# NSA attention: adding the causal mask with VectorE in PSUM in place of mask products on TensorE

## The chip, the cores and the metric

The kernel runs on 1 core of one Trainium2 chip. The metric is the device time of one execution in microseconds, as the median of several runs.

## The reference, cut to what matters

The program is two transformer blocks in a row, all in float32, on 256 tokens (plus 256 context tokens in the second block) with width 1024. The change touches only the NSA mixer of the first block, and of that only the part with full scores: the selected branch and the window branch. With 256 tokens, four blocks of 64 keys and a top-4 choice, every block is chosen, and the window of 512 covers everything. So both branches are plain causal attention over the 256 keys, each with keys and values of its own:

```python
def _masked_softmax(s, mask):
    s = jnp.where(mask, s.astype(jnp.float32), -1e30)
    m = jnp.max(s, axis=-1, keepdims=True)
    p = jnp.where(mask, jnp.exp(s - m), 0.0)
    return p / jnp.maximum(jnp.sum(p, axis=-1, keepdims=True), 1e-30)
...
        ss = jnp.einsum('bqgrd,bgqkld->bqgrkl', qb, k_g).reshape(...) * scale
        ps = _masked_softmax(ss, mask_s).reshape(...)          # mask_s: kpos <= t
...
        pw = _masked_softmax(jnp.einsum('bqgrd,bkgd->bqgrk', qb, kwb) * scale, mask_w)
        o_win = jnp.einsum('bqgrk,bkgd->bqgrd', pw, vwb)
        return gb[..., 0:1] * o_cmp + gb[..., 1:2] * o_slc + gb[..., 2:3] * o_win
```

There are 16 query heads of 64 dimensions in 2 key/value groups. The second block has four mixers' code, of which two layers run: a GQA attention and an MLA attention, both without a mask.

## The kernel before, in words

The program is one block per engine (TensorE, ScalarE, VectorE, GpSimd, and SyncE for the loads), written out by hand. Engines meet by semaphores; each engine runs its instructions in the order in which they are written. The program is cut into phases, and at the end of each (`end_phase`) TensorE, ScalarE and VectorE wait for one another. Weights stream from memory into six slots of SBUF.

One helper, `attention`, exists once per engine (L723 for TensorE, L1386 for ScalarE, L1865 for VectorE) and is called for NSA, GQA and MLA. Its unit is a `Pair`: two heads (`e` = 0, 1) and one tile of 128 queries. In NSA there are 16 pairs: 4 groups of heads `j`, 2 key/value groups `u`, and 2 query tiles `qt`. A pair has two branches (selected and window), and its width per branch is `w = 128 * (qt + 1)`: an even pair (qt = 0) has 2 heads x 2 branches x 128 keys = 512 scores a row, an odd one (qt = 1) has 2 x 2 x 256 = 1024. Below they are the short and the wide pair. Each head has a PSUM bank of its own: pair p uses banks 0 and 1 if p is even, 2 and 3 if it is odd.

For step p the engines do, each in this order:

- TensorE: the scores of pair p (waits until the exponentials of pair p-2 have left the banks, `att_exp`), then the transposes of the probabilities of pair p-2 (L739; waits for `att_scaled` of it and for `att_PT` of the pair before it, which frees banks 4 and 5), then the products with the values of pair p-3 (L1021, and L1025 for the compressed branch; waits for `att_PT`).
- VectorE: the row maximum of pair p, read from both banks in one instruction (L1873; waits for `att_S`), then for pair p-1 the reciprocal of the sums, the gate and four multiplications (L1881, L1884, L1889), and after every second pair a copy of the output (L2151).
- ScalarE: the exponentials of pair p, four instructions with their sums (L1397; waits for `att_max`), then the copy of the transposed probabilities of pair p-2 from PSUM to SBUF (L1406; waits for `att_T`).

The mask: only the last 128 keys of each branch are on the diagonal. `scores` makes the score product (L1009) with `stop=False`, and then, for each head, multiplies the constant `mneg` (0 where key <= query, -1e30 elsewhere) with the identity, repeated for the two branches, onto the diagonal block of the same bank (L1013). A float32 product is two instructions in the trace, so L1009 and L1013 have four each per pair. The constant `trix` is 1 where row < column and 0 elsewhere; it lies in SBUF already. `NEG` is -1e30.

Of the kernel before, what the change touches and what calls it, by code (L numbers as in the profile page):

```python
# [18 lines left out]
ALU = mybir.AluOpType  # L19
# [3 lines left out]
P = 128  # L23
# [6 lines left out]
NEG = -1e30  # L30
# [155 lines left out]
def build(nc, dr):  # L186

    with ExitStack() as ctx:
# [6 lines left out]
        banks = ctx.enter_context(nc.psum_tensor("bank", [P, 8, 512], F32))  # L195
# [22 lines left out]
        def C(name, rows=P):  # L218
            o, w = CO[name]
            return consts[0:rows, o:o + w]  # L220
# [4 lines left out]
        def slot(s, w=SLOTW):  # L225
            return ring[:, s * SLOTW:s * SLOTW + w]
# [26 lines left out]
        ident, ones = C("ident"), C("ones")  # L253
# [79 lines left out]
        kk = [pl(2, T) for _ in range(NKV)]  # L333
# [9 lines left out]
        q_all = pl(KD, T)  # L343
# [24 lines left out]
        start = pl(NE)  # L368
# [239 lines left out]
        def _(pe):  # L608
# [3 lines left out]
            mm, tr = nc.tensor.matmul, nc.tensor.transpose  # L612
# [20 lines left out]
            def dot(out, lhs, rhs, k):  # L633

                for i in range(k):
                    last = mm(out, lhs(i), rhs(i), start=i == 0, stop=i == k - 1)  # L636
                return last
# [36 lines left out]
            def hn_block(k):  # L674
                pe.wait_ge(s["hn_ready"], n["hn_ready"] - KD + k + 1)
                return hn[:, k, :]
# [75 lines left out]
            for v in range(VT):  # L752
                r = min(P, VR - v * P)
                last = tr(bank[v][:, 0:r], vec_rows[0:r, v, :], ident[0:r, 0:r])
# [130 lines left out]
            for c in range(2):  # L885
                last = dot(bank[5][:, c * 80:(c + 1) * 80], lambda k: hn_block(k)[:, c * P:(c + 1) * P],
                           lambda k: w_small[:, k, :], KD)
# [30 lines left out]
            def kvw(sl, x):  # L918
                return lambda k: slot(sl)[:, k * 384 + x * P:k * 384 + (x + 1) * P]
# [7 lines left out]
            for br in range(2):  # L927
                for t in range(TT):
                    last = dot(bank[2][:, (br * 2 + t) * P:(br * 2 + t + 1) * P], lambda k: hn[:, k, t * P:(t + 1) * P],
                               kvw(3, 2 * br), KD)  # L930
# [6 lines left out]
            for g in range(NKV):  # L937
# [3 lines left out]
                last = mm(bank[g][:, :], dup, k_roped[:, 1:3, :], start=True, stop=True)  # L941
# [3 lines left out]
            for x in range(2):  # L945
                landed(1 - x)
                for hb in range(2):
                    o = (x * 2 + hb) * 2 * NCMP
                    last = dot(bank[7][:, o:o + 2 * NCMP],
                               lambda k: slot(1 - x)[:, k * HID + hb * P:k * HID + hb * P + P],  # L950
                               lambda k: blk[x][:, k, :], 16)
# [6 lines left out]
            for g in range(NKV):  # L958
                last = dot(bank[4][0:NCMP, 320 + g * DH:320 + (g + 1) * DH],
                           lambda k: hid[:, 2 + k, g * NCMP:(g + 1) * NCMP], lambda k: w_cmp2[:, k, P:P + DH], 2)  # L960
# [42 lines left out]
            def nsa_pair(j, u, qt):  # L1003
                w = P * (qt + 1)

                def scores(*out):
                    for e in range(2):
                        rows = slice(64 * e, 64 * e + 64)
                        mm(out[e][:, 0:2 * w], q_all[rows, 2 * j + u, qt * P:(qt + 1) * P], kk[u][rows, :, 0:w],  # L1009
                           start=True, stop=False)  # L1010
                    for e in range(2):
                        diag = out[e][:, 0:2 * w].rearrange("p (b k) -> p b k", b=2)[:, :, qt * P:w]
                        last = mm(diag, C("mneg"), ident.unsqueeze(1).to_broadcast([P, 2, P]), start=False, stop=True)  # L1013
                    return last

                def values(out, pt):
                    to = [out[64 * e:64 * e + 64, qt * P:(qt + 1) * P] for e in range(2)]
                    for x in range(2 * (qt + 1)):
                        br, kt = x // (qt + 1), x % (qt + 1)
                        for e in range(2):  # L1020
                            mm(to[e], v_tok[:, br, kt, u * DH:(u + 1) * DH], pt[:, e, x * P:(x + 1) * P],  # L1021
                               start=x == 0, stop=False)
                    for e in range(2):
                        c = (4 * u + 2 * e + qt) * P
                        last = mm(to[e], v_cmp[0:NCMP, u, :], ct[0:NCMP, j, c:c + P], start=False, stop=True)  # L1025
                    return last

                return Pair(scores, values, tiles=[x * P for x in range(2 * (qt + 1))])
# [12 lines left out]
            for t in range(TT):  # L1041
                last = dot(bank[0][:, t * 36:(t + 1) * 36], lambda k: hn[:, k, t * P:(t + 1) * P],
                           lambda k: w_route[:, k, :], KD)
            last.then_inc(s["route_pe"], 1)
            for t in range(TT):
                for k in range(KD):
                    last = tr(bank[2 + 2 * t + k // 4][:, (k % 4) * P:(k % 4 + 1) * P], hn[:, k, t * P:(t + 1) * P], ident)
# [88 lines left out]
            for l in range(2):  # L1136
                norm(T2)
                if l == 0:

                    landed(0)  # L1140
                    for t in range(4):
                        last = dot(bank[6 + t // 2][:, (t % 2) * T:(t % 2 + 1) * T], lambda k: hn_block(k)[:, t * P:(t + 1) * P],
                                   lambda k: slot(0)[:, k * T:(k + 1) * T], KD)
# [58 lines left out]
                else:  # L1202

                    landed(0)
                    for b in range(3):
                        last = dot(bank[1 + b][:, 0:T], lambda k: slot(0)[:, k * 384 + b * P:k * 384 + (b + 1) * P],
                                   lambda k: hn_block(k)[:, 0:T], KD)
# [72 lines left out]
                w = T2 if l == 0 else T  # L1280
# [463 lines left out]
        def _(ve):  # L1744
# [3 lines left out]
            V = nc.vector  # L1748
# [116 lines left out]
            def attention(pairs, per, done, output):  # L1865

                N = len(pairs)
                for p in range(N + 4):
                    if p < N:
                        u = pairs[p]  # L1870
                        x = 2 * (p % 2)
                        ve.wait_ge(s["att_S"], done + p + 1)
                        V.tensor_reduce(nmax[p % 3][:, :, 0:u.branches],  # L1873
                                        banks[:, x:x + 2, 0:u.branches * u.w].rearrange("p e (b k) -> p e b k", b=u.branches),
                                        AX.X, ALU.max, negate=True).then_inc(s["att_max"], 1)
                    if 1 <= p < N + 1:
                        t = p - 1
                        u = pairs[t]
                        ve.wait_ge(s["att_exp"], 2 * (done + t + 1))
                        fac = pfac[t % 3][:, :, 0:u.branches]  # L1880
                        V.reciprocal(fac, psum_[t % 3][:, :, 0:u.branches])  # L1881
                        ve.drain()
                        if u.gate is not None:
                            V.tensor_tensor(fac, fac, u.gate, ALU.mult)  # L1884
                            ve.drain()
                        for e in range(2):
                            for b in range(u.branches):
                                pb = probs[t % 3][:, e, b * u.w:(b + 1) * u.w]
                                last = V.tensor_scalar(pb, pb, fac[:, e, b:b + 1], None, ALU.mult)  # L1889
                        last.then_inc(s["att_scaled"], 1)  # L1890
                    if p >= 4 and (p - 4) % per == per - 1:
                        g = (p - 4) // per
                        ve.wait_ge(s["att_O"], done + p - 3)
                        output(g, bank[6 + g % 2]).then_inc(s["att_ev"], 1)
# [185 lines left out]
            for x, name in enumerate(("cmp_pe_k", "cmp_pe_v")):  # L2080
                pe_cols = cols[:, VO[name]:VO[name] + 16]
                for g in range(NKV):
                    src = bank[5 + x][:, g * T:(g + 1) * T].rearrange("p (c j) -> p j c", j=STRIDE)
                    for h in range(2):
                        rows = slice(64 * h, 64 * h + 64)
# [60 lines left out]
            def nsa_pair(j, u, qt):  # L2146
                gate = gsel[:, j, 8:24].rearrange("p (b n) -> p n b", b=2)[:, 4 * u + qt:4 * u + qt + 3:2, :]
                return Pair(branches=2, w=P * (qt + 1), gate=gate)

            attention([nsa_pair(j, u, qt) for j in range(4) for u in range(2) for qt in range(2)], 2, 0,  # L2150
                      lambda g, b: V.tensor_copy(o_t[:, g // 2 + 4 * (g % 2), :], b[:, 0:T]))  # L2151
            end_phase()
# [144 lines left out]
            for i in range(ITEMS + 2):  # L2297
# [6 lines left out]
                if i < ITEMS:  # L2304
                    x = i % 2
# [23 lines left out]
            for l in range(2):  # L2329
# [4 lines left out]
                if l == 0:  # L2334
# [24 lines left out]
                    for b in range(2):  # L2359
                        block_step(b, KVG)  # L2360
                    end_phase()
                    attention([Pair(branches=1, w=512 if t % 4 < 2 else 256) for t in range(32)], 4, 16,
                              lambda g, b: V.tensor_copy(o2[:, g, :], b))
                    end_phase()
                    gemm(2, 4, T2, 16, 1)
                else:
# [36 lines left out]
                    with ve.Fori(1, 4) as trip:  # L2403
                        for q in range(2):
                            heads(trip * 2 + q, q)
                    heads(8, 0)
                    end_phase()
                    attention([Pair(branches=1, w=512) for _ in range(16)], 2, 48,
                              lambda g, b: V.tensor_copy(o2x[:, g, :], b[:, 0:T]))
                    end_phase()  # L2410
                    gemm(2, 4, T, 16, 2)
                w = T2 if l == 0 else T
# [192 lines left out]
```

## Time and profile before

| | us |
|---|---|
| median of 3 runs | 2266.38 (2265.53 to 2266.64) |
| profiled execution, its own time | 2266.16 |
| its span, first to last instruction | 2264.4 |
| TensorE busy in the span | 2047.4 (90%) |
| VectorE busy | 1050.3 (46%) |
| ScalarE busy | 550.6 (24%) |
| mean granted TensorE clock, share of full | 0.951 |

Busy time is the time in which an engine executed something. The chain that ended last is followed back from the last instruction: at each step to what released it, or to the instruction before it on its engine; its shares say on which engine time went by. NSA attention fills the stretch from 494.6 to 568.6 us of the span.

### The profile page before, as it was taken

To read this page: it belongs to the slowest core of one execution; us is meant where nothing else is said; L and a number is where in the kernel's file an instruction comes from. 1 tells how busy PE (TensorE), PEld (TensorE's weight loads), DVE (VectorE), ACT (ScalarE), POOL (GpSimd) and SP (SyncE) were. 2 spreads that over 40 slices of the span, in tenths; PEclk is the share of its full clock that TensorE was granted. 3 is DMA by queue.
4 is the path that set the end of the run, shared out by engine and by line. 5 is a ranking of instruction groups with operands and counts; after the bars stand their busy time and mean duration, and the time that the engine had idled before them with its cause. 6 is when DMAs were issued, how large, how long until landed. Compare 5 with 4: busy or idle time off the path is not lost.

```text
span 2264.4 us, 27759 instructions
## 1 busy us (share of the span) xinstructions
PE 2047.4 (90%) x10184; PEld 1448.1 (64%) x10184; DVE 1050.3 (46%) x2090; ACT 550.6 (24%) x1095; POOL 61.4 (3%) x69
## 2 busy tenths in 40 slices
PE   6999897878986999997978979999999878999997
PEld 4888686855874555554435448888644445678886
DVE  3456565535722222223666247777697423523311
ACT  3333300025012111112136213323100123534410
POOL 0000000000000000000000001111000010000000
PEclk9999999689988999998989989999999989999999
DMA  9444465040453999951000102222476011034451
GB/s 386 154 183 186 182 272 233 19 186 1 186 227 140 425 424 422 420 207 79 0 38 1 56 19 93 82 84 93 187 278 243 36 35 61 1 114 158 154 198 44
DMA packets 39081, 357.13 MB, mean 158 GB/s; under 512 B 4295, under 2 KB 8526, under 8 KB 9934
## 3 DMA queue, kind: packets, MB, share of 16 engines
q1 hardware_dynamic: 38990, 355.91, 40.1%
q8 instruction: 59, 0.97, 0.2%
q14 instruction: 32, 0.26, 0.0%
HBM read 354.84 MB, written 1.05 MB: 157 GB/s over the span
## 4 chain that ended last, share of the span: by engine, by line
PE 80%; DVE 6%; ACT 4%; PEld 3%; issue 3%; DMA 2%; PEldq 1%; DVEq 1%; SPq 0%; ACTq 0%
PE bank L636 42%; PE bank L1290 12%; PE bank L1097 6%; PEld bank L636 3%; PE bank L1083 3%; PE bank L1119 3%; PE bank L739 2%; DMA ring<-in_ada 2%; PE bank L662 2%; PE bank L1262 1%; ACT ring L1397 1%; DVE ring L1873 1%; ACT ring L1406 1%; DVE rstd L1805 1%; ACT hn L1369 1%
## 5 line engine op out<-in xcount | busy, mean ns | idle before, releaser
L636 PE MATMUL bank<-hn,ring 128*128 128x256 f32 (+1 forms) x2080 | 524.4, 413 | 14.8 <-ACT hn L1369 9.7
L636 PE MATMUL bank<-arena,ring 128*128 128x256 f32 (+3 forms) x1728 | 499.9, 450 | 29.5 <-issue 12.0
L636 PEld LDWEIGHTS bank<-hn,ring 128*128 128x128 f32 x2080 | 402.3, 194 | 125.1 <-issue 67.7
L636 PEld LDWEIGHTS bank<-arena,ring 128*128 128x128 f32 (+1 forms) x1728 | 329.7, 201 | 196.5 <-issue 153.2
L1290 PE MATMUL bank<-hn,ring 128*128 128x256 f32 x704 | 161.0, 382 | 6.2 <-ACT hn L1369 6.2
L1290 PEld LDWEIGHTS bank<-hn,ring 128*128 128x128 f32 x704 | 134.6, 191 | 25.6 <-issue 7.0
L1785 DVE SCALAR_TENSOR_TENSOR bank<-ring,c_rows 128x1024 f32<-128x1024 f32 x96 | 118.2, 1231 | 36.6 <-DMA ring<-in_ada 31.5
L1290 PE MATMUL bank<-ring 128*128 128x256 f32 x528 | 124.0, 385 | 5.9 <-DVEq L2505 5.9
L1858 DVE SCALAR_TENSOR_TENSOR resid<-bank,ada,resid 128x256 f32 x56 | 25.6, 482 | 198.4 <-PE bank L636 197.8
L1785 DVE SCALAR_TENSOR_TENSOR ring<-ring,c_rows 128x1024 f32<-128x1024 f32 x96 | 117.2, 1221 | 0.0
L1290 PEld LDWEIGHTS bank<-ring 128*128 128x128 f32 x528 | 102.2, 194 | 21.0 <-issue 6.6
L1357 ACT ACTIVATE hn<-resid 128x256 f32<-128x256 f32 (+1 forms) x64 | 30.0, 493 | 351.6 <-DVE resid L1858 343.8
L2303 DVE COPY ring<-bank 128x128 f32<-128x128 f32 x39 | 11.4, 292 | 209.1 <-PE bank L1104 209.1
L1873 DVE TENSOR_REDUCE ring<-bank 128x2 f32<-128x1024 f32 (+2 forms) x64 | 65.6, 1025 | 85.2 <-PE bank L1013 29.5
L1397 ACT ACTIVATE ring<-bank,ring 128x512 f32<-128x512 f32 (+2 forms) x160 | 84.2, 535 | 78.9 <-DVE ring L1873 77.5
L2488 DVE SCALAR_TENSOR_TENSOR ring<-bank,cols,ring 128x255 f32<-128x255 f32 x88 | 40.5, 480 | 93.2 <-ACT ring L1685 89.5
L2441 DVE TENSOR_TENSOR ring<-ring,bank 128x256 f32<-128x256 f32 x154 | 60.0, 419 | 46.9 <-PE bank L1290 36.8
L739 PEld LDWEIGHTS bank<-consts,ring 128*128 128x128 f32 x416 | 46.9, 145 | 54.0 <-issue 51.2
L739 PE MATMUL bank<-consts,ring 128*128 128x128 f32 x416 | 60.1, 285 | 22.0 <-ACT ring L1406 20.6
L1083 PE MATMUL bank<-ring,arena 64*128 64x256 f32 x624 | 77.9, 388 | 1.8 <-ACT arena L1584 1.8
L1119 PE MATMUL bank<-ring 128*64 128x512 f32 x312 | 75.5, 605 | 0.0
L1662 ACT ACTIVATE ring<-ring,cols 128x512 f32<-128x512 f32 x44 | 35.8, 814 | 161.8 <-DVE ring L2441 161.8
(376 smaller groups left out, 2185.9 us busy)
## 6 DMA issues: line engine op xcount, KB each, us to landing
ring<-in_ada SPq DMA_DIRECT2D x28, 2048.0 KB, 10.4
ring<-in_up SPq DMA_DIRECT2D x44, 1024.0 KB, 4.9
ring<-in_egu SPq DMA_DIRECT2D x20, 2048.0 KB, 10.6
ring<-in_edn SPq DMA_DIRECT2D x39, 1024.0 KB, 9.2
ring<-in_down SPq DMA_DIRECT2D x16, 1408.0 KB, 10.0
arena<-in_egu SPq DMA_DIRECT2D x10, 2048.0 KB, 10.4
hn<-in_egu SPq DMA_DIRECT2D x9, 2048.0 KB, 10.6
ring<-in_adat SPq DMA_DIRECT2D x8, 2048.0 KB, 12.4
```

The lines of the kernel that those rows point to most:

```text
L636: last = mm(out, lhs(i), rhs(i), start=i == 0, stop=i == k - 1)
L662: last = mm(bank[7][:, 0:w], ones, hn[:, k, 0:w], start=k == 0, stop=k == KD - 1)
L739: last = tr(bank[4 + e][:, x * P:(x + 1) * P], probs[t % 3][:, e, c:c + P], ident)
L1083: last = mm(moe_sum(4 * half + m), y_sb[v % 2][rows, m * P:(m + 1) * P], s_t[v % 2][rows, :], start=v == 0 and m % 2 == 0, stop=v == ITEMS ...
L1097: last = mm(bank[x][64 * q:64 * q + 64, 0:T], x_t[x][:, k, :], w_gate_up(i % 4)[:, k * 512 + q * T:k * 512 + (q + 1) * T], start=k == 0, s ...
L1119: last = mm(bank[6 + x][64 * half:64 * half + 64, :], he_t[:, x, k * CAP:(k + 1) * CAP], w_down(v % 4)[:, k * D + half * 512:k * D + half ...
L1290: last = mm(bank[4 * q + b][:, 0:T], lhs[:, k, :], rhs(k), start=k == 0, stop=k == 3)
L1397: last = fn(probs[p % 3][:, e, o:o + u.w], banks[:, 2 * (p % 2) + e, o:o + u.w], ACT.Exp, bias=nmax[p % 3][:, e, b:b + 1], accum_out=psum_ ...
L1785: V.scalar_tensor_tensor(products, w, 1.0, c_row if layer == 0 else c_rows[:, v, :], ALU.mult, ALU.mult, accum_out=sums[x][:, b, v:v + 1])
L1873: V.tensor_reduce(nmax[p % 3][:, :, 0:u.branches], banks[:, x:x + 2, 0:u.branches * u.w].rearrange("p e (b k) -> p e b k", b=u.branches), ...
L2441: V.tensor_tensor(out, one, other, ALU.add).then_inc(s["up_added"], 1)
L2488: V.scalar_tensor_tensor(aa, uu, cols[:, ds(j + (cw + tap * 2 * FB + x * FB), 1)], aa, ALU.mult, ALU.add)
```

## The change

The products with the mask leave TensorE: the score product now closes its own accumulation. VectorE, when the scores of an NSA pair are there, adds `trix * NEG` to the two diagonal blocks of each head, in place in PSUM, one instruction per head of 256 elements a row. Then it drains, and then takes the maximum as before. For the pairs of GQA and MLA (`branches` = 1) nothing is changed.

```diff
                 def scores(*out):
                     for e in range(2):
                         rows = slice(64 * e, 64 * e + 64)
-                        mm(out[e][:, 0:2 * w], q_all[rows, 2 * j + u, qt * P:(qt + 1) * P], kk[u][rows, :, 0:w],
-                           start=True, stop=False)
-                    for e in range(2):
-                        diag = out[e][:, 0:2 * w].rearrange("p (b k) -> p b k", b=2)[:, :, qt * P:w]
-                        last = mm(diag, C("mneg"), ident.unsqueeze(1).to_broadcast([P, 2, P]), start=False, stop=True)
+                        last = mm(out[e][:, 0:2 * w], q_all[rows, 2 * j + u, qt * P:(qt + 1) * P], kk[u][rows, :, 0:w],
+                                  start=True, stop=True)
                     return last
...
                         ve.wait_ge(s["att_S"], done + p + 1)
+                        if u.branches == 2:
+                            for e in range(2):
+                                diag = banks[:, x + e, 0:2 * u.w].rearrange("p (b k) -> p b k", b=2)[:, :, u.w - P:u.w]
+                                V.scalar_tensor_tensor(diag, C("trix").unsqueeze(1).to_broadcast([P, 2, P]), NEG, diag,
+                                                       ALU.mult, ALU.add)
+                            ve.drain()
                         V.tensor_reduce(nmax[p % 3][:, :, 0:u.branches],
```

## Rows read from the trace of the kernel before

**Rows 1.** The page: the chain that ended last, shares of the span by line.

```profile
PE bank L636 42%; PE bank L1290 12%; PE bank L1097 6%; PEld bank L636 3%; PE bank L1083 3%; PE bank L1119 3%; PE bank L739 2%; DMA ring<-in_ada 2%; PE bank L662 2%; PE bank L1262 1%; ACT ring L1397 1%; DVE ring L1873 1%; ACT ring L1406 1%; DVE rstd L1805 1%; ACT hn L1369 1%
```

**Rows 2.** The chain in NSA's steady part: start us, us, what.

```profile
504.99 1.07 PE bank L1013 x4
...
506.09 1.24 DVE ring L1873
...
517.70 0.92 ACT ring L1406
...
518.76 0.63 PE bank L739 x4
519.39 1.02 PE bank L1021 x16
...
520.77 1.06 PE bank L1009 x4
...
555.52 1.07 PE bank L1013 x4
```

**Rows 3.** The same chain at the start of NSA attention.

```profile
495.85 2.00 PE bank L1013 x4
497.85 1.67 PE bank L1009 x4
499.52 1.07 PE bank L1013 x4
```

**Rows 4.** Timeline of one round: start us, us, engine, line, operation, shapes, [idle before <-releaser].

```profile
516.93 0.42 DVE L2151 COPY arena<-bank 128x256 f32<-128x256 f32 x1
518.03 0.69 DVE L1873 TENSOR_REDUCE ring<-bank 128x4 f32<-128x512 f32 x1 [0.69 <-PE bank L1013]
518.76 0.30 PE L739 MATMUL bank<-consts,ring 128*128 128x128 f32 x1 [0.77 <-ACT ring L1406]
...
520.14 0.61 ACT L1406 ACTIVATE ring<-bank 128x512 f32<-128x512 f32 x1
```

**Rows 5.** Timeline of VectorE elsewhere: operations near to the new ones.

```profile
1092.38 0.43 DVE L2349 TENSOR_TENSOR arena<-arena,consts 128x256 f32<-128x256 f32 x1
1092.72 0.42 DVE L2351 TENSOR_TENSOR arena<-bank,consts 128x256 f32<-128x256 f32 x1
1093.21 0.43 DVE L2353 TENSOR_TENSOR arena<-arena 128x256 f32<-128x256 f32 x1
...
443.28 0.35 DVE L2121 TENSOR_TENSOR arena<-bank,consts 128x60 f32<-128x60 f32 x2 [0.67 <-PE bank L989]
```

**Rows 6.** Groups by line and shape: xcount | busy us, mean ns | idle before.

```profile
L1785 DVE SCALAR_TENSOR_TENSOR bank<-ring,c_rows 128x1024 f32<-128x1024 f32 x96 | 118.2, 1231 | 36.6 <-DMA ring<-in_ada 31.5 <-PEq L617 0.3 <-issue 0.2
L1858 DVE SCALAR_TENSOR_TENSOR resid<-bank,ada,resid 128x256 f32 x56 | 25.6, 482 | 198.4 <-PE bank L636 197.8 <-issue 0.6
```

**Rows 7.** Windows: stretch, its length, busy us of PE, PEld, DVE, ACT, POOL, granted clock, DMA.

```profile
558.42:563.90 5.48, 3.03 (x22) 2.40 (x24) 2.52 (x11) 2.90 (x9) 0.00 (x0) 0.69 0.00 0
712.87:718.90 6.03, 3.67 (x33) 2.71 (x33) 0.00 (x0) 0.60 (x1) 1.22 (x2) 1.00 0.00 0
...
1906.93:1912.60 5.67, 3.46 (x4) 1.41 (x5) 2.27 (x4) 3.49 (x9) 0.00 (x0) 0.66 0.00 0
...
560.50:563.90 3.40, 3.03 (x22) 2.40 (x24) 0.98 (x4) 0.82 (x2) 0.00 (x0) 0.50 0.00 0
```

**Rows 8.** The chain behind the idle time at 558.4 us.

```profile
560.87 1.09 PE bank L739 x4
561.96 1.91 PE bank L1021 x16
```

**Rows 9.** Windows: the whole start, the steady part, and the phase behind NSA attention.

```profile
494.62:499.05 4.43, 4.43 (x12) 2.18 (x12) 0.69 (x1) 0.30 (x2) 0.00 (x0) 0.50 0.00 0
504.99:555.45 50.46, 45.88 (x360) 29.65 (x360) 28.76 (x91) 29.76 (x111) 0.00 (x0) 1.00 0.00 1
...
568.60:625.70 57.10, 56.31 (x256) 48.13 (x256) 44.79 (x86) 5.25 (x9) 0.00 (x0) 1.00 0.46 185
```

## The prediction

> **What bounds the kernel now.** I read the page's chain first, then the chain inside NSA attention, then the timeline of one round, then the windows with the granted clock. Over the whole program the chain lies on TensorE's projections; the lines that the change touches are a small part of it [rows 1]. What the edit is worth is therefore read from NSA attention, 494.6 to 568.6 us.
>
> There the chain is a loop through three engines, once per round of a short and a wide pair [rows 2]: mask product of the wide pair (L1013) 1.07 us, its maximum on VectorE 1.24, exponentials on ScalarE until 517.70, copy L1406 0.92, transposes of the next short pair (L739) 0.63, value products 1.02 for L1021 and the short L1025, score product of the next wide pair (L1009) 1.06, and again L1013. L1013 stands in the loop seven times, first at 504.99, last at 555.52; six rounds take 50.53 us, so a round is 8.42 us. The short pair's mask product is not in the loop: behind it TensorE waits 0.77 us for the copy L1406 [rows 4]. No engine is full by itself: in 50.46 us TensorE is busy 45.88, VectorE 28.76 and ScalarE 29.76 [rows 9].
>
> **The part removed.** For a wide pair TensorE's mask product is 1.07 us of the loop; all of it goes, since the maximum starts 0.03 us behind it, at 506.09 [rows 2]. For a short pair another 1.07 us goes from TensorE, but off the loop. At the start the removal is worth more: the clock is at 0.50 of full, that is 1.2 GHz, up to 499.05 [rows 9], and the chain holds both pairs' products one behind the other: 2.00 + 1.67 + 1.07 us, so that the wide pair's maximum can begin at 500.6 [rows 3].
>
> **The part added.** Two SCALAR_TENSOR_TENSOR of 256 elements and a drain, before each maximum. The trace has no such instruction with input and output in the same PSUM bank. The nearest rows are two operations of 256 elements, one reading PSUM and a constant, then a drain, then a dependent operation: first to second start 0.34 us, second to the dependent one 0.49 [rows 5]. Sum 0.83, and I take 0.84. Writing to PSUM adds nothing visible: 1024 elements into a bank take 1.231 us [rows 6], as much as the read of 1024 by the maximum, 1.24 [rows 2]. Low bound: the pair of 60 elements, 0.35 us, with the same 0.07 us of drain (0.49 less the 0.42 of L2351) [rows 5], 0.42. High bound: both instructions as long as the form with a scalar from memory, 0.48 us [rows 6], so 2 x 0.06 more, 0.95. Should an update in place in one bank run at half rate, it would be about twice 0.84, 1.7; nothing in the trace points to it.
>
> The Trainium skill ("VectorE: DVE Perf Modes", section "The DRAIN you can't avoid") says that the next operation does not start until the pipe has emptied. By that, the second instruction would start after the first one's whole 0.43 us, the addition would be 0.92, and the sum below 0.6 us worse. The row has it start at 0.34, so the row is kept.
>
> **What lies where.** Wide pair: the maximum hangs on L1013 directly, so the addition starts as soon as L1009 ends: 1.07 goes, 0.84 comes, 0.23 us per round. Seven rounds: 1.6 us. Short pair: the scores are ready up to 2 x 1.07 us earlier, but VectorE is busy with the wide pair until the copy at 516.93 ends, 517.35. Shifted by 0.23 that is 517.12; plus 0.84 the short maximum starts at 517.96, against 518.03 - 0.23 = 517.80 if nothing but the loop had moved [rows 4]. So it is 0.16 us late relative to the loop. Behind its exponentials ScalarE makes the next copy, which ends at 520.75 [rows 4]. The transposes that need it will come where L1013 stands now, 520.77 + 1.06 = 521.83 [rows 2]. That is 1.1 us of slack; 0.16 of it is used, so the short pair's addition is hidden, and without this cover it would cost up to 0.84 a round. Queued behind VectorE's wait for the scores are the scalings L1889 of the pair before; TensorE needs them over a microsecond later still. No DMA and no queue of SyncE or GpSimd is moved.
>
> Start: without masks the two score products take 1.22 us (494.62 to 495.85) and, at half clock, twice 1.06 = 2.12, so they end at 497.96. With 0.84 the wide maximum starts at 498.8 in place of 500.6: 1.8 us. The last pairs behind 556 change nothing else.
>
> Together 1.8 + 1.6 = 3.4 us less, if the clock stays. It is passed on: the next phase is TensorE's, at 56.31 of 57.10 us busy with DMA share 0.46 [rows 9], and its loads wait for slots that TensorE frees.
>
> **The clock.** TensorE's order is wide scores, transposes, values, short scores, and then the wait for copy L1406. All the removed work gathers there: 0.77 + 2 x 1.07 - 0.23 = 2.7 us of gap, some 2.5 of them seen as idle, in every round. The trace of before has six idle times of TensorE between 2.0 and 2.6 us. After four of them, at 558.42, 1171.22, 1899.47 and 1906.93, a stretch at 0.50 (1.2 GHz) follows; after two, at 712.87 and 1818.76, none. Two of the four and one of the two are shown, the others repeat them [rows 7]. The one at 558.42 is of this very stage: 2.44 us idle, then 3.40 us at 0.50. Its price stands behind it: transposes 1.09 us for 0.63, values 1.91 for 1.02 [rows 8, 2], that is 0.46 + 0.89 = 1.4 us per stretch, and 1.7 (half of 3.40) if it covers score products too. The wait L1406 is in the loop, and what follows it is the loop's TensorE part, so nothing hides this.
>
> The idle time comes seven times before the one at 558.42, which is there already. If two in three are followed by a low stretch it is 4 or 5, and the first low stretch shifts the next, so I take 4: 4 x 1.4 = +5.6 us.
>
> The Trainium skill ("TensorE: Matmul & The Clock Gate", section "A second HAM failure mode: psum-queue depth-cycling") speaks against the change as well: short idle times between groups of products, if frequent, make the clock go down and up, and the throughput falls. The trace agrees in the row at 558.42; that the steady part as it is stays at 1.00 with gaps of 0.77 us [rows 9] says that small gaps do not do it.
>
> **The rivals.** (A) Forecast: clock lost in part of the rounds. -3.4 + 5.6 = +2.2 us: 2266.16 + 2.2 = 2268.4 for the profiled execution, which lies 0.2 below the median, so 2268.6. With 2 to 5 low stretches, -0.6 to +3.6: 2265.8 to 2270.0.
>
> (B) The clock holds, or falls once: -3.4 to -2.0, 2263.0 to 2264.4. For it: the two idle times without a fall, and a whole steady part at 1.00. Against: the idle time would be triple what it is now. With the addition at its low bound of 0.42, another 8 x 0.42 = 3.4 us: 2259.6.
>
> (C) Slower: the clock falls after every idle time, seven times, and once more in the start: 8 x 1.4 - 3.4 = +7.8, 2274.2. It decides from 6 stretches on (6 x 1.4 - 3.4 = +5.0). For it: four of six. Against: TensorE, running at half rate, closes the gap of the next rounds in part.
>
> (D) The addition in place costs 1.7 us. Each round is then 1.7 - 1.07 = 0.63 longer, the start 0.9 better instead of 1.8: 7 x 0.63 - 0.9 = +3.5, with shorter idle times and so fewer falls, say two: +6.3, 2272.7.
>
> That the change does not do what it says has no room: the same sum reaches the same bank, and VectorE's drain orders it before the maximum.
>
> **How the numbers follow.** A 0.60, B 0.20, C 0.13, D 0.07. A measurement of this kernel can tell about 0.2% from no change, 4.5 us: 2261.9 to 2270.9. All of A and nearly all of B lie inside; C and D lie mostly above it. Faster by over 0.2%: 0.04 (B with the low bound). Slower: 0.17. Within: 0.79. The range takes in B without its low bound and goes up into D and the edge of C: 2262.8 to 2272.6, leaving out about one in seven.
>
> **What would show it.** In the profile after: L1013 and `mneg` are gone; 32 new VectorE instructions of about 0.43 us, and 0.84 us from the end of L1009 to L1873. A round at full clock is 8.2 us. One idle time of TensorE of about 2.5 us per round, before L739, ended by L1406. In the windows, three to five stretches at 0.50 between 505 and 556 us, each followed by a round of some 9.6 us. The wide maximum of the first round near 498.8. I am wrong if the granted clock stays at 1.00 from 500 to 556 (then B), if the two additions take over 1.2 us (D), or if the short maximum becomes what TensorE waits for.

## The result, and the profile after

| us | before | after |
|---|---|---|
| median | 2266.64 (2265.53 to 2268.14, 5 runs) | 2277.33 (2272.21 to 2281.05, 5 runs) |
| profiled execution | 2266.16 | 2272.21 |
| NSA attention in it | 73.98 | 83.63 |
| granted clock in NSA attention | 0.95 | 0.71 |

The change makes the kernel slower: ratio 1.0042, 95% interval 1.0028 to 1.0057; the medians are 10.7 us apart. I had predicted 2268.6 with a range up to 2272.6.

NSA attention, below also "the stage", means here: from TensorE's first product in it to TensorE's first product of the next phase (before 494.62 to 568.60, after 495.50 to 579.13). It grew by 9.65 us; the rest of the profiled execution became 3.6 us shorter (more on that with e12 and e13). The profiled execution of after is the shortest of its five.

The page of after: span, busy times, and the granted clock in 40 slices (NSA attention is the end of slice 9, slice 10 and the start of slice 11, counted from 1).

```profile
span 2270.4 us, 27679 instructions
...
PE 2047.1 (90%) x10120; PEld 1446.4 (64%) x10120; DVE 1061.9 (47%) x2122; ACT 550.6 (24%) x1095; POOL 61.1 (3%) x69
...
PEclk9999999677997999998989989999999989999999
```

TensorE has lost the 64 instructions of the mask products and yet is busy as long as before (2047.1 against 2047.4 us). VectorE has gained 11.6 us. The slow part must be a rate.

The windows of after: stretch, length, busy us of PE, PEld, DVE, ACT, POOL with their instructions, granted clock, DMA share and GB/s. First the whole of NSA attention, then five stretches in a row.

```profile
495.50:579.13 83.63, 66.71 (x416) 41.01 (x417) 50.11 (x152) 38.89 (x144) 0.00 (x0) 0.71 0.00 1
...
510.40:517.15 6.75, 6.75 (x36) 4.15 (x34) 2.84 (x9) 1.99 (x9) 0.00 (x0) 0.50 0.01 2
517.20:520.55 3.35, 1.76 (x18) 0.91 (x16) 3.12 (x11) 2.84 (x9) 0.00 (x0) 1.00 0.01 2
520.60:524.00 3.40, 3.32 (x24) 2.58 (x24) 1.49 (x7) 1.99 (x9) 0.00 (x0) 0.50 0.00 0
524.05:530.80 6.75, 4.23 (x36) 2.49 (x32) 5.05 (x15) 3.19 (x11) 0.00 (x0) 1.00 0.00 0
530.90:537.60 6.70, 6.70 (x36) 4.09 (x36) 2.91 (x7) 1.54 (x8) 0.00 (x0) 0.50 0.00 1
```

Before, the whole stretch had 0.95, and its steady part 1.00 [rows 9]. Now the clock goes between 2.4 GHz and 1.2 GHz in every round: stretches at 0.50 begin at 510.4, 520.6, 530.8, 541.1, 551.3, 561.5 and 571.8 us, four of them some 6.8 us long and three 3.4. The low clock with which the stage begins lasts until 506.9, before until 499.05 [rows 9]. Together it is 49 us at 0.50 in this stage, against 7.8 before.

What TensorE did before a fall is in its timeline (start, busy, line, operation; in brackets the idle time before it and who ended it):

```profile
530.40 0.69 PE L739 MATMUL bank<-consts,ring 128*128 128x128 f32 x4 [2.52 <-ACT ring L1403]
```

The transposes of the short pair wait 2.52 us for ScalarE's copy, where before they waited 0.77 [rows 4]. Four tenths of a microsecond behind the end of that wait the clock is at 0.50. This wait is one of the two longest: ahead of the seven falls TensorE waits 1.32, 1.72, 2.52, 1.57, 1.65, 2.52 and 2.08 us, so most are shorter than 2.5, and yet the clock falls within 0.6 us of the end of each.

The chain of waits through NSA attention of after, the start and one round (start, length, what; DVEq is VectorE's queue, here its drain). L1009 is the score product, `bank` the PSUM that TensorE writes to, L1873 the addition, L1876 the maximum, L1394 the exponentials, L1403 the copy, L1018 and L1022 the value products:

```profile
495.50 2.96 PE bank L1009 x8
...
498.48 0.43 DVE bank L1873
498.91 0.33 DVEq L1875
...
499.31 1.23 DVE ring L1876
...
533.61 2.03 PE bank L1009 x4
...
536.50 1.24 DVE ring L1876
...
538.13 1.56 ACT ring L1394 x7
539.69 0.92 ACT ring L1403
...
540.75 0.80 PE bank L739 x4
541.55 1.91 PE bank L1018 x16
543.46 0.62 PE bank L1022 x4
544.08 2.03 PE bank L1009 x4
```

Beside the chain of before the ScalarE and VectorE pieces are unchanged (the addition apart), and TensorE's are longer, most of them nearly doubled: score product 2.03 for 1.06, values 1.91 for 1.02 and, in the compressed branch, 0.62 for 0.36, transposes 0.80 for 0.63. Together 0.97 + 0.89 + 0.26 + 0.17 = 2.3 us. This round takes 544.08 - 533.61 = 10.47 us, where the sum of the prediction has 8.42 - 0.23 = 8.2 at full clock: 2.3 us more. A round is from here on the time from one wide pair's score product to the next.

So the 9.65 us come together: up to the second wide score product 7.49 us for 9.24 (-1.8); six rounds 61.11 for 50.60 (+10.5: the masks' 6 x -0.23 and the clock's +11.9); the end 15.03 for 14.14 (+0.9).

### The profile page after: what moved, and what is told of

It is laid out like the page before. It is cut to its first block, busy times and chain, and to the rows that moved or that the text cites. A ratio compares the mean times of both kernels' runs of the same rounds, so it can differ in the third digit from the quotient of the medians.

```text
span 2270.4 us, 27679 instructions
## 1 busy us (share of the span) xinstructions
PE 2047.1 (90%) x10120; PEld 1446.4 (64%) x10120; DVE 1061.9 (47%) x2122; ACT 550.6 (24%) x1095; POOL 61.1 (3%) x69
## 4 chain that ended last, share of the span: by engine, by line
PE 80%; DVE 6%; ACT 4%; PEld 3%; issue 3%; DMA 2%; DVEq 1%; PEldq 1%; SPq 0%; ACTq 0%
PE bank L636 42%; PE bank L1287 12%; PE bank L1094 6%; PEld bank L636 3%; PE bank L1080 3%; PE bank L1116 3%; PE bank L739 2%; DMA ring<-in_ada 2%; PE bank L662 2%; PE bank L1259 1%; ACT ring L1394 1%; DVE ring L1876 1%; ACT ring L1403 1%; DVE rstd L1802 1%; PEldq L627 1%
## 5 line engine op out<-in xcount | busy, mean ns | idle before, releaser
L636 PE MATMUL bank<-hn,ring 128*128 128x256 f32 (+1 forms) x2080 | 523.6, 412 | 14.3 <-ACT hn L1366 9.7
L1394 ACT ACTIVATE ring<-bank,ring 128x512 f32<-128x512 f32 (+2 forms) x160 | 84.2, 534 | 88.8 <-DVE ring L1876 88.1
L739 PEld LDWEIGHTS bank<-consts,ring 128*128 128x128 f32 x416 | 51.1, 155 | 69.1 <-issue 64.9
L1876 DVE TENSOR_REDUCE ring<-bank 128x2 f32<-128x1024 f32 (+2 forms) x64 | 65.6, 1025 | 57.5 <-PE bank L1182 29.3
L739 PE MATMUL bank<-consts,ring 128*128 128x128 f32 x416 | 66.2, 304 | 28.6 <-ACT ring L1403 27.4
## 6 DMA issues: line engine op xcount, KB each, us to landing
ring<-in_ada SPq DMA_DIRECT2D x28, 2048.0 KB, 10.3
```

Source lines behind the costliest of these rows:

```text
L739: last = tr(bank[4 + e][:, x * P:(x + 1) * P], probs[t % 3][:, e, c:c + P], ident)
L1394: last = fn(probs[p % 3][:, e, o:o + u.w], banks[:, 2 * (p % 2) + e, o:o + u.w], ACT.Exp, bias=nmax[p % 3][:, e, b:b + 1], accum_out=psum_ ...
L1876: V.tensor_reduce(nmax[p % 3][:, :, 0:u.branches], banks[:, x:x + 2, 0:u.branches * u.w].rearrange("p e (b k) -> p e b k", b=u.branches), ...
```

## The experiments

Two theories. The clock theory: the products that left were not needed for the result, but they filled TensorE's waiting; without those of the short pairs its clock falls. The VectorE theory: the additions, above all those of the short pairs, disturb the order of VectorE's queue or cost more than their duration, and the clock is a side effect. All medians are beside runs of before on the same chip (median 2267.26 for e1 to e4, 2267.70 for e5 to e8, 2268.22 for e9 to e11).

### e1 and e2: one kind of pair at a time

e1 moves only the wide pairs' mask to VectorE, e2 only the short pairs' (the same edit with the two conditions exchanged). The lines of e1 against after:

```diff
+                                  start=True, stop=qt != 0)
+                    if qt == 0:
+                        for e in range(2):
...
+                        if u.branches == 2 and u.w == 2 * P:
```

> The mask of wide pairs is added by VectorE, that of short pairs stays a product on TensorE. Clock theory: the round is as short as that of the change at full clock (8.2 us), but TensorE's idle time is 0.77 + 1.07 - 0.23 = 1.6 us instead of 2.5, too short to lose the clock: stretches at 0.50 inside the steady part none or one, time 2266.6 - 3.4 = 2263.2 us (2262.5 to 2265). VectorE theory (the additions in PSUM lengthen the path): half of the additions, so about half of the loss, 2272 us.

> The other half: VectorE adds the mask of short pairs, wide pairs keep the product. Clock theory: the loop keeps its 1.07 us product, so nothing is gained per round (8.42 us), and the idle time is 0.77 + 1.07 = 1.84 us, between 1.6 and 2.5: if it holds the clock 2265 to 2266.6 us, if it loses it in part 2268 to 2272. VectorE theory: the short pair's addition is the late one, so nearly the whole loss is here, 2275 us.

e1: 2268.04 (11 runs), ratio 1.0007 (0.9998 to 1.0016). e2: 2280.58 (5 runs), ratio 1.0057 (1.0044 to 1.0070). Windows of e1 (stage, steady part), and TensorE's timeline in a steady round:

```profile
495.37:568.21 72.84, 58.00 (x449) 35.69 (x449) 44.37 (x136) 38.29 (x144) 0.00 (x0) 0.94 0.00 1
504.00:556.00 52.00, 42.90 (x352) 26.64 (x350) 35.29 (x110) 30.83 (x119) 0.00 (x0) 1.00 0.01 1
```

```profile
535.71 0.63 PE L739 MATMUL bank<-consts,ring 128*128 128x128 f32 x4 [1.46 <-ACT ring L1407]
```

The wide half of the change does what the sum said: steady rounds of 8.20 us, 0.23 less than before, at a clock of 1.00, though the idle time has gone from 0.77 to 1.46 us. In the profiles the whole loss is in the short half, which is off the loop in time but not in the clock: in e2 the clock falls four times, rounds take 9.3 to 10.3 us in place of 8.4, the stage 80.1. Its median is 3.3 us above that of the whole change, and the intervals of the two ratios overlap. By its time alone e2 spoke for the VectorE theory (2275 expected, and at most 2272 by the clock theory); e7 decides that. e1's stage is 1.1 us shorter than before's, yet its median, expected at 2263.2, does not show it: the profile is of the shortest of its eleven executions, and five others took 2270.6 to 2272.4 us. e2's profile is likewise of its shortest (2273.58; the other four took 2277.9 to 2282.3).

### e3 and e6: the whole change, with TensorE's gap filled

Before the score product of a short pair TensorE makes two products of `mneg` (e3) or one (e6, `range(1)`) into the same banks. `start=True` of the score product overwrites them, so they are waste. VectorE does all that it does in after.

```diff
                 def scores(*out):
+                    if qt == 0:
+                        for e in range(2):
+                            mm(out[e][:, 0:2 * P], C("mneg"), ident.unsqueeze(1).to_broadcast([P, 2, P]), start=True, stop=True)
```

> The whole change (all 32 additions on VectorE), and in addition TensorE makes the old mask products of the short pairs before their score product, which then overwrites them: filler, off the loop. Clock theory: idle time 1.6 us as in the run with wide pairs only, clock 1.00, 2263.2 us (2262.5 to 2265), so more work gives 14 us less than the change. VectorE theory: no better than the change, 2277 us or more.

> The whole change with one filler product (two instructions, 0.53 us) before each short score product: idle time 2.0 us, between the 2.5 of the change and the 1.5 of the run with two. If the loss grows with the idle time: 2270 to 2276 us. If it has a step: 2267 or 2277 us.

e3: 2267.48 (11 runs), 1.0002 (0.9993 to 1.0011): the loss is gone, though 2263.2 was expected. e6: 2270.66 (11 runs), 1.0018 (1.0009 to 1.0027), between the two, as expected for a loss that grows with the idle time. Windows and timeline of e3:

```profile
507.00:557.00 50.00, 41.48 (x346) 26.15 (x346) 38.09 (x116) 29.37 (x109) 0.00 (x0) 1.00 0.01 1
```

```profile
528.32 0.63 PE L739 MATMUL bank<-consts,ring 128*128 128x128 f32 x4 [1.47 <-ACT ring L1406]
```

Steady rounds of 8.21 us, with all 32 additions on VectorE. So the short pair's addition is hidden, as predicted. What e3 lacks of the expected gain is in part the price of the filling itself: in the first pair nothing runs beside it, so its two waste products, at half clock, put off the first score product by 2.0 us, and the low stretch of the start is followed by one more at 503.3.

```profile
495.26 2.07 PE L1009 MATMUL bank<-consts 128*128 128x256 f32 x4 [1.19 <-ACTq L1346]
```

With one product (e6) the idle time is 1.89 us. After the first of the two shown the clock holds, after the next it falls (timeline and window of e6):

```profile
526.87 0.63 PE L739 MATMUL bank<-consts,ring 128*128 128x128 f32 x4 [1.89 <-ACT ring L1406]
...
535.08 0.63 PE L739 MATMUL bank<-consts,ring 128*128 128x128 f32 x4 [1.89 <-ACT ring L1406]
```

```profile
536.55:546.70 10.15, 10.15 (x46) 5.47 (x44) 4.76 (x14) 3.42 (x11) 0.00 (x0) 0.50 0.00 0
```

### e4 and e7: no mask at all, and no mask for short pairs

e4 is after without the addition and its drain: the mask is left out. e7 is before without the short pairs' mask product: that mask is left out, VectorE is as in before.

```diff
-                        if u.branches == 2:
...
-                            ve.drain()
```

```diff
+                           start=True, stop=qt == 0)
+                    if qt == 0:
+                        return last
```

> The mask is left out altogether: neither the products nor the additions (scores above the diagonal enter the softmax). It prices the additions. The loop is 8.42 - 1.07 = 7.35 us a round at full clock, the start 2.6 us shorter, and the idle time 0.77 + 2 x 1.07 - 1.07 = 1.84 us. Clock theory: without falls 2266.6 - 10.1 = 2256.5 us, with a fall in every round 2266. VectorE theory: 2256.5 us, clock at 1.00.

> The kernel before without the mask of the short pairs (it is left out there): no VectorE instruction is added, 1.07 us of product per round goes from beside the loop, idle time 1.84 us. Clock theory: as slow as the run in which VectorE adds the short masks, 2280 us. VectorE theory (that run is slow because of its additions): 2265 us.

e4: 2259.27 (6 runs), 0.9967 (0.9955 to 0.9980). A round is 7.37 us at full clock, 0.83 less than 8.20: that is what the addition costs on the loop. The idle time is 1.69 us in five rounds, and the clock falls in two of them. e7: 2277.26 (6 runs), 1.0046 (1.0030 to 1.0062), as slow as the change, although VectorE does nothing new and a part of the work is left out. Windows of e7 (stage; the stretch behind one of its idle times) and its timeline:

```profile
495.70:575.70 80.00, 64.59 (x449) 40.12 (x449) 38.09 (x120) 38.19 (x144) 0.00 (x0) 0.84 0.00 1
520.60:527.40 6.80, 6.80 (x32) 4.02 (x31) 0.27 (x3) 1.28 (x7) 0.00 (x0) 0.50 0.00 0
```

```profile
520.14 0.68 PE L739 MATMUL bank<-consts,ring 128*128 128x128 f32 x4 [1.83 <-ACT ring L1408]
520.75 1.98 PE L1023 MATMUL bank<-ring,arena 128*64 128x128 f32 x16
...
523.28 2.08 PE L1009 MATMUL bank<-arena,ring 64*128 64x512 f32 x4
```

The rounds of e7 are those of e2 within 0.1 us (9.94, 9.61, 10.31, 9.18, 9.78, 10.31 against 9.92, 9.65, 10.32, 9.25, 9.79, 10.31). With and without the short addition on VectorE the clock falls at the same places and the rounds are the same: the VectorE theory falls.

### e5 and e8: the clock held, and the addition doubled

e5 is e1 with e3's two waste products. e8 is e5 with each wide addition made twice, a drain behind each pair of them.

```diff
-                            for e in range(2):
+                            for e in (0, 1, 0, 1):
...
+                                if e == 1:
+                                    ve.drain()
```

> VectorE adds the mask of wide pairs only; short pairs keep their product on TensorE and TensorE makes two more mask products before them, which the score product overwrites. TensorE's idle time before the transposes is then 1.6 - 1.07 = 0.5 us. Clock theory (idle time of TensorE decides): rounds of 8.2 us, no low stretch in the steady part in any execution, so the executions that took up to 2272 us with 1.6 us of idle time are gone: 2263.5 us, 2262.5 to 2265. Rival (1.6 us is harmless, and the long executions lose the clock elsewhere in the program): 2268 us again, with the same spread.

> As the run with 0.5 us of idle time, but the additions of the wide pairs are made twice, each with its drain. It prices an addition while the clock holds: 0.83 us per round, 8 times, so 6.6 us above that run, 2270.1 us, idle time 1.4 us. If the additions were hidden or clock losses came from VectorE: less than 2 us or over 10 us above it.

e5: 2273.41 (12 runs), 1.0019 (1.0009 to 1.0029), a miss (expected 2263.5). Its steady part is as expected, 1.00 with rounds of 8.21 and an idle time of 0.40. As in e3, the first pair's waste products cost 2.0 us of the start. The larger loss lies behind the steady part (a window and the timeline of e5):

```profile
561.95:579.00 17.05, 15.31 (x77) 11.58 (x78) 7.23 (x17) 3.76 (x4) 0.00 (x0) 0.50 0.00 1
```

```profile
562.95 1.09 PE L739 MATMUL bank<-consts,ring 128*128 128x128 f32 x4 [3.16 <-ACT ring L1410]
563.97 1.98 PE L1025 MATMUL bank<-ring,arena 128*64 128x128 f32 x16
...
566.49 1.97 PE L739 MATMUL bank<-consts,ring 128*128 128x128 f32 x8
...
573.39 6.46 PE L636 MATMUL bank<-arena,ring 128*128 128x256 f32 x16 [0.74 <-PEq L617]
```

In the last round no scores follow, so TensorE waits 3.16 us, and the clock falls. Here it stays at 1.2 GHz for 17 us, though TensorE is almost always busy, with transposes and value products of 64 columns; it rises only 5.6 us into the dense products of the next phase. In e1 the same place had one stretch of 3.4 us, and there the clock rose while TensorE ran the same transposes and value products. So the end of the stage is a second place where the clock counts, and that stretch was in before too [rows 7].

e8: 2273.83 (6 runs), 1.0030 (1.0018 to 1.0042). Chain of e8, one round's beginning:

```profile
525.53 1.08 PE bank L1012 x4
...
526.64 0.43 DVE bank L1880
527.07 0.33 DVEq L1883
...
527.48 0.43 DVE bank L1880
527.90 0.33 DVEq L1883
...
528.31 1.24 DVE ring L1884
```

A round is 9.04 us, 0.83 more than e5's 8.21: the second addition costs exactly its own time. The rounds alone make 7 x 0.83 = 5.8 us, and 6.6 above e5's median was expected; it is just 0.4 above. By that run's own measure (less than 2 us: hidden) the median missed; the rounds show that the addition is not hidden. The long stretch at the end did not come in the profiled execution, only one of 3.4, which would make up for most of it; that the other executions are alike is not shown.

### e9, e10 and e11: the end of the stage filled

Behind the last scores TensorE makes waste products into banks whose exponentials are done: four of them in e9 (on e1) and e10 (on e5), three in e11 (on before, with nothing moved to VectorE).

```diff
+                    if p == N and tail:
+                        pe.wait_ge(s["att_exp"], 2 * (done + N - 1))
+                        for e in range(tail):
+                            mm(bank[e % 2][:, 0:2 * P], C("mneg"), ident.unsqueeze(1).to_broadcast([P, 2, P]), start=True, stop=True)
```

> VectorE adds the mask of wide pairs only, and behind the last score product TensorE makes four filler products (2.1 us) into the banks of the last short pair, whose exponentials have been read. The idle time before the last short transposes falls from 3.15 to about 1 us. Theory: in the run with wide pairs only, the executions near 2272 us lose the clock at this place and then run transposes, value products and the start of the next phase at half rate, as the profile of the run with 0.5 us of idle time shows (17 us at 0.50 from 561.9 on). Then no low stretch begins between 556 and 572 us, the stage is 1.4 us shorter than the 72.8 us of that run, and the executions near 2272 us are gone: median 2263 us, all under 2267. Rival (the long executions lose the clock in the steady part): median 2268 and the old spread.

> The run with 0.5 us of idle time in the rounds, with the same four filler products at the end. Tail theory: that run's low stretch of 17.1 us is gone, the stage is 75.4 - 6 = 69 to 71 us, the median falls from 2273.4 to 2264 to 2267 us. If the steady part or the rest of the program were the cause, it stays at 2273.

> The kernel before with three filler products (1.6 us) behind the last score product; nothing else. Idle time there 2.46 - 1.6 = 0.9 us. Tail theory: the low stretch of 3.4 us at 560.5 is gone, 1.4 us less: 2265.2 us. Without influence: 2266.6 us.

| kernel | median | ratio, interval | stage |
|---|---|---|---|
| e9 | 2265.77 (11 runs) | 0.9987 (0.9978 to 0.9997) | 71.2 |
| e10 | 2266.17 (11 runs) | 0.9991 (0.9982 to 1.0000) | 73.2 |
| e11 | 2262.49 (7 runs) | 0.9970 (0.9959 to 0.9981) | 72.6 |

Windows of e11 (stage, its end) and the timeline where the filling stands:

```profile
496.60:569.20 72.60, 65.22 (x486) 41.52 (x487) 38.40 (x120) 38.90 (x144) 0.00 (x0) 0.97 0.00 1
556.00:572.00 16.00, 14.13 (x117) 10.22 (x116) 7.65 (x21) 6.19 (x13) 0.00 (x0) 1.00 0.00 1
```

```profile
560.35 1.56 PE L735 MATMUL bank<-consts 128*128 128x256 f32 x6
562.88 0.63 PE L743 MATMUL bank<-consts,ring 128*128 128x128 f32 x4 [0.97 <-ACT ring L1410]
```

In all three the clock stays at 1.00 through the end of the stage, and e10 has e5's long stretch no more; its median is as expected (2264 to 2267), and its stage, counted from the first score product as in its expectation, takes 71.2 us. e9 missed: 2263 with all executions under 2267 was expected, and three of eleven took 2268.4 to 2269.3; e1's group at 2270.6 to 2272.4 is gone. e11 was expected at 2265.2. It is the fastest kernel of the study that keeps the mask and beats e9 and e10: its median is 5.7 us less than before's, and its slowest execution (2263.27) is shorter than the shortest of the 23 of before beside it (2264.69), from three products that nobody reads, six instructions in the trace. Its own stage accounts for 1.4 us of that. The two profiled executions are only 3.1 us apart; in e11 the part ahead of the stage is 2.0 us longer, and what makes up for it is elsewhere, in code that is the same (windows of before, then of e11: from the start of the last value products to the first product of L1097, which is L1101 in e11; the last 300 us of the span):

```profile
567.50:715.20 147.70, 119.39 (x498) 95.44 (x498) 68.00 (x182) 22.46 (x43) 1.14 (x2) 0.88 0.43 173
1963.70:2264.40 300.70, 276.44 (x1305) 237.77 (x1303) 71.96 (x154) 80.08 (x123) 0.00 (x0) 0.98 0.35 126
```

```profile
568.10:713.90 145.80, 117.55 (x500) 94.32 (x499) 68.01 (x182) 22.47 (x43) 1.15 (x3) 0.89 0.44 175
1962.30:2261.30 299.00, 274.75 (x1304) 236.58 (x1302) 72.01 (x154) 80.13 (x123) 0.00 (x0) 0.98 0.35 126
```

The same instructions take 1.9 and 1.7 us less, each with less time at 0.50 (30.7 for 34.1 us, 12.6 for 14.3). That the filled gap at 560 us causes this is not shown. From the stage's end on, e11's profile takes 1692.1 us and before's two take 1695.8 and 1695.6, but the changed kernel, with no gap filled, takes 1691.3 in one of its profiles and 1695.9 in the other. Where e11's median gets the rest of its gain was not settled.

### e12 and e13: before and after once more

> The kernel before, a second execution in the profile. If the gain of the run with the closed tail (4 us more than the 1.4 us that the first profile's low stretch of 3.4 us costs) comes from the tail, the low stretch behind the last scores is longer here than 3.4 us (up to 17, as in one of the runs). If not, the stage takes 74.0 us again and the difference lies in the rest of the program.

> The changed kernel, a second execution in the profile. Theory (every idle time of 2.5 us costs the clock, whatever the alignment): again a low stretch in each round, rounds of 9.3 to 10.7 us, the stage 83 to 85 us. If the first profile was a chance, fewer than five low stretches and a stage under 80 us.

One execution each: 2268.56 and 2280.49 us, 11.9 apart. Window of NSA attention in e12, then in e13:

```profile
497.00:571.10 74.10, 65.09 (x480) 41.52 (x480) 38.45 (x121) 38.99 (x145) 0.00 (x0) 0.95 0.00 1
```

```profile
497.20:582.90 85.70, 68.95 (x417) 42.52 (x417) 50.13 (x153) 38.94 (x145) 0.00 (x0) 0.68 0.00 1
```

The stage is 11.6 us longer, so it holds nearly all of the difference, and again a stretch at 0.50 stands in every round (511.8, 522.0, 532.3, 542.5, 552.7, 563.0, 573.2), the last of them 13.7 us long. The pattern is no chance of one execution. What does vary is the rest: up to TensorE's first product of the stage, the same instructions take 493.8 to 497.6 us in the 15 profiles of this study, with 87.1 to 94.6 us at 0.50. Of the 8.3 us between the two profiled executions of after, 1.7 lie ahead of the stage, 2.0 in it and 4.6 behind it. So one profiled execution (2272.21) can lie 5 us below the median of its kernel (2277.33).

### All kernels side by side

Idle time: TensorE's, ahead of the short pair's transposes, in steady rounds behind a stretch at full clock. The stage begins with TensorE's first product in it, a waste product in e3, e5, e6, e8 and e10.

| kernel | idle, us | clock in steady rounds | rounds, us | stage, us |
|---|---|---|---|---|
| e5 | 0.40 | 1.00 | 8.21 | 77.4 |
| before | 0.77 | 1.00 | 8.42 | 74.0 |
| e8 | 1.24 | 1.00 | 9.04 | 80.5 |
| e1, e3 | 1.46 | 1.00 (e3: one more fall in the start) | 8.20, 8.21 | 72.8, 73.8 |
| e4 | 1.69 | two falls | 7.37 at full clock, up to 8.3 | 66.8 |
| e2, e7 | 1.83 | three falls, one more in the start | 9.2 to 10.3 | 80.1, 80.0 |
| e6 | 1.89 | one fall, one more at the end | 8.2 to 10.5 | 77.7 |
| after | 2.52 (two; the others, behind a slow stretch, 1.3 to 2.1) | a fall in every one | 9.3 to 10.7 | 83.6 |

## Why the prediction was wrong

**The sum at full clock: right.** The removal at the start was put at 1.8 us: the first wide maximum comes 3.81 us into the stage in place of 6.0, so 2.2, of which the longer low clock of the start takes 0.4 back up to the second wide score product. The addition was put at 0.84; the chain has 0.83 from L1873 to L1876, e8 pays 0.83 for a second one, and e4 gains 0.83 by having none. Its high case of 1.7 (D) is excluded. The 0.92 that the prediction worked out beside it took the Trainium skill ("VectorE: DVE Perf Modes", section "The DRAIN you can't avoid") too strictly: the section adds that a next operation that is not held starts earlier. The trace shows 0.83. The round of 8.2 us is there in e1 and e3. The cover of the short pair's addition is there in e3.

**The idle time: right in place and cause, in size only at full clock.** Predicted some 2.5 us in every round, ahead of L739, ended by the copy. The trace has 2.52 in two of seven rounds; in the others, behind a slow stretch, it has 1.32 to 2.08.

**How often the clock falls: wrong.** This is the step that failed first. I took two falls in three idle times, from six cases of the whole program, and let the first fall shift the next, so four in the seven rounds ahead of the fall that was there already. It falls in every round: six new falls, and the low stretch of the start is 6.8 us longer. The shift is real (behind a slow stretch the next idle time is 1.72 or 1.57 us, not 2.52, since TensorE's part ends later) but did not save a fall: at 520.6 and 541.1 us the clock fell all the same.

```profile
520.68 1.09 PE L739 MATMUL bank<-consts,ring 128*128 128x128 f32 x4 [1.72 <-ACT ring L1403]
...
540.75 0.80 PE L739 MATMUL bank<-consts,ring 128*128 128x128 f32 x4 [1.57 <-ACT ring L1403]
```

The six cases were also a poor sample: single waits, five of them in other code, where what the change makes is one wait repeated every 10 us. Behind the 1.7 to 2.0 us of e2 and e7 the clock fell about every second time. The length of the wait is not what decides: the waits of 1.3 to 1.7 us in after each had a fall, while 1.46 us in e1 had none, and behind 2.46 us at the end of e2's stage the clock held at 1.00. What makes after lose it each time stays open.

```profile
568.94 0.63 PE L739 MATMUL bank<-consts,ring 128*128 128x128 f32 x4 [2.46 <-ACT ring L1407]
```

**What a fall costs: wrong.** The 1.4 us came from the stretch at 560.5 to 563.9, in the last round, where only transposes and value products follow [rows 8]. In the middle the score product of the wide pair follows and is in the loop too (+0.97, and +0.26 for the value products of the compressed branch), and more than half of the stretches are twice as long. Six rounds lost 11.9 us, 2.0 each, against 1.4. In the terms of the sum: -1.8 for the start (its longer low clock included), -1.4 for the rounds' masks, +11.9 for six falls in place of +5.6 for four, and +0.9 for the end of the stage, which had no term; together the 9.65 us of the stage. The rival with a fall in each round (C) named the mechanism and had 0.13; with its 1.4, and eight falls, it gave 2274.2, 3 us short. The median lies above the range, which ended at 2272.6, because both errors go the same way; the profiled execution, 2272.21, lies inside it only because its part behind the stage was short.

**The rule I had against the change.** The rows show a stretch at 0.50 in each round, at idle times of 1.32 to 2.52 us. The Trainium skill ("TensorE: Matmul & The Clock Gate", section "A second HAM failure mode: psum-queue depth-cycling") says of one bf16 kernel that frequent short idle times between groups of products make the clock go down and up, at a cost in throughput. The trace of this float32 kernel agrees, and I had quoted it; I gave it too few rounds.

## What to carry to other kernels

Before work is taken off TensorE, look at where its waiting will gather and at the granted clock behind waits of that size; price a fall at half rate on everything of TensorE that is in the loop behind it, for every round. A product that is off the critical path may be what keeps the clock up, and where a wait can't be shortened, products that nobody reads can fill it: three of them at one place gave 0.30% here. They are free only where TensorE waits anyway; ahead of the first pair they cost 2.0 us. Read a stage's length in a profile beside the median of several runs, since the rest of the program moves by some microseconds of its own.

## What was unexpected of the hardware

- Idle times of 1.46 us in each round left the clock at 1.00 (e1, e3); behind 1.69 to 1.89 us it fell in some rounds and held in others (e2, e4, e6, e7), in one kernel and with the same idle time; and in after it fell at 1.32 us. So the idle time alone does not decide.
- Once down, the clock can stay down through work that keeps TensorE busy: 17.05 us in e5 and 13.7 in e6 and e13, over transposes and value products and 4 to 6 us of projections. In before and e1 the stretch at the same place was 3.4 us, over the same kind of work. No run here shows what makes the difference.
- Filling one gap went with less time at 0.50 in unchanged code up to 1400 us behind it (e11, one profile, and after's first profile is as short there without it). What stays open is why e11's median is some 4 us below what its stage accounts for, and those of e1, e2, e5 and e7 2 to 7 us above; of e1 and e2 the profile shows the shortest execution.
